# Attention of a two-layer streaming encoder: the reciprocal row sums are repeated on ScalarE and transposed as one block

## What is computed

```python
def sink_softmax(logits, sink):
    m = jnp.maximum(jnp.max(logits, axis=-1, keepdims=True), sink)
    p = jnp.exp(logits - m)
    return p / (jnp.sum(p, axis=-1, keepdims=True) + jnp.exp(sink - m))
...
    s_band = jnp.einsum('bnqcgd,bnscd->bncgqs', qb, kb).astype(jnp.float32) * scale + b_band
    s_band = jnp.where(valid[None, :, None, None, None, :], s_band, -jnp.inf)
```

## Time and profile before

| | |
|---|---|
| Runs | 2971.2 us median of 3 (2969.07 to 2971.53) |
| The profiled execution, its own time | 2970.41 us |
| Its span | 2968.6 us |
| TensorE products busy | 2883.8 us, 97% of the span |
| VectorE, ScalarE, GpSimd busy | 1532.7, 679.5 and 916.9 us |
| Attention of layer 0, of layer 1 | some 178 to 382 us, some 1632 to 1968 us from the start of the span |

### The profile page before, as it was taken

One profiled execution on the slowest core, in us unless ns is written; L12 is line 12 of the kernel. 1 busy time (PEld: TensorE's weight loads), 2 busy tenths in 40 slices (PEclk: granted clock), 3 DMA queues, 4 the chain that ended last, 5 costly groups with the idle time before them and its releaser, 6 DMA issues. The chain is left out here.

```text
span 2968.6 us, 47619 instructions
## 1 busy us (share of the span) xinstructions
PE 2883.8 (97%) x18423; PEld 2706.7 (91%) x18423; DVE 1532.7 (52%) x2815; ACT 679.5 (23%) x1327; POOL 916.9 (31%) x860
## 2 busy tenths in 40 slices
PE   8999999999999999999887999999999999999998
PEld 6987799999999999998487877789999999999997
DVE  5146624544444444455688777532644444444445
ACT  4035521000000000013467655532100000000002
POOL 4233333222222222224033754323222222222221
PEclk8999999999999999999999999999999999999998
DMA  4430011111111111114012000021111111111111
GB/s 123 66 96 10 22 29 36 36 36 42 42 42 42 42 42 42 36 43 130 1 35 72 11 10 9 20 80 37 37 42 42 42 37 41 42 42 38 39 36 74
DMA packets 178204, 129.78 MB, mean 44 GB/s; under 512 B 25313, under 2 KB 168353, under 8 KB 177846
## 3 DMA queue, kind: packets, MB, share of 16 engines
q1 hardware_dynamic: 178066, 127.90, 15.2%
HBM read 111.13 MB, written 15.16 MB: 43 GB/s over the span
## 5 line engine op out<-in xcount | busy, mean ns | idle before, releaser
L1215 POOL CAST w_hi<-w_raw 128x1024 fp32r<-128x1024 f32 x120 | 145.1, 1209 | 1111.8 <-PE ps_gemm L1450 606.9
L666 DVE TENSOR_TENSOR h<-h,ps_gemm 128x1170 f32<-128x1170 f32 x192 | 263.7, 1373 | 398.1 <-PE ps_gemm L1466 210.6
L1450 PE MATMUL ps_gemm<-xh,w_hi 128*128 128x390 f32 x1920 | 448.5, 341 | 0.0
L1450 PE MATMUL ps_gemm<-xh,w_lo 128*128 128x390 f32 x1920 | 448.1, 342 | 0.0
L1450 PE MATMUL ps_gemm<-xl,w_hi 128*128 128x390 f32 x1920 | 446.1, 340 | 0.0
L1450 PEld LDWEIGHTS ps_gemm<-xh,w_hi 128*128 128x128 f32 x1920 | 352.2, 189 | 0.1
L1450 PEld LDWEIGHTS ps_gemm<-xl,w_hi 128*128 128x128 f32 x1920 | 349.4, 189 | 0.0
L1450 PEld LDWEIGHTS ps_gemm<-xh,w_lo 128*128 128x128 f32 x1920 | 349.1, 189 | 0.0
L1218 POOL TENSOR_TENSOR w_lo<-w_raw,w_hi 128x1024 fp32r<-128x1024 f32 x120 | 289.5, 2413 | 17.4
L674 ACT ACTIVATE ac<-ac 128x1184 f32<-128x1184 f32 x44 | 52.5, 1194 | 863.2 <-DVE ac L731 863.2
L1414 PE MATMUL ps_gemm<-xl,w_hi 128*128 128x390 f32 x1056 | 246.5, 342 | 0.0
(11 more groups left out here) (411 smaller groups left out, 4716.1 us busy)
## 6 DMA issues: line engine op xcount, KB each, us to landing
w_raw<-in_w_gate SPq DMA_DIRECT2D x44, 512.0 KB, 3.8
w_raw<-in_w_up SPq DMA_DIRECT2D x44, 512.0 KB, 3.8
w_raw<-in_w_down SPq DMA_DIRECT2D x44, 512.0 KB, 3.5
w_raw<-in_w_in_b SPq DMA_DIRECT2D x13, 512.0 KB, 4.0
w_raw<-in_w_qkv_a SPq DMA_DIRECT2D x10, 512.0 KB, 4.0
residual_park<-h SPq DMA_DIRECT2D x1, 4680.0 KB, 13.6
h<-residual_park SPq DMA_DIRECT2D x8, 585.0 KB, 7.4
out<-yt SPq DMA_DIRECT2D x9, 512.0 KB
```

The costliest lines, as they stand in the source:

```text
L666: dve.tensor_tensor(c3(h[:, m, :]), c3(h[:, m, :]), pse(j), ALU.add).then_inc(evac[j % 2], 1)
L1215: pool.tensor_copy(whi[c % 3][:], raw[c % 2][:]).then_inc(w_hi_done, 1)
L1450: mm = pe.matmul(ps[j % 2][:, m_, 0:CH], w[:, k, :], x[:, k, m_ * CH:(m_ + 1) * CH], start=(k == 0 and w is wh and x is XH), stop=(k == KT ...
```

## The change

ScalarE gets a new instruction per unit: it repeats the two columns of reciprocals 64 times each into a tile of 128x128 (`ri_a` in layer 0, `ri_b` in layer 1, two buffers each), in step i+1 for unit i, between the first and the second exponential of unit i+1. TensorE transposes that tile as one block in place of the two products, and waits for `p_wide` in place of `p_rinv`. VectorE waits, before it overwrites reciprocals, for the copy made three units earlier. The five memsets of `ca` go from VectorE, step 4, to GpSimd, step 3, behind the sinks of unit 3 and ahead of the split of unit 0; VectorE waits for them at the end of step 7.

```diff
-             ("ptb_h", [P, 512], F32)],
+             ("ptb_h", [P, 512], F32), ("ri_b", [P, 2, 2, HD], F32)],
...
-             ("kts_a", [P, 2, 160], F32), ("sbias_a", [P, 2, 160], F32)],
+             ("kts_a", [P, 2, 160], F32), ("sbias_a", [P, 2, 160], F32), ("ri_a", [P, 2, 2, HD], F32)],
...
+        def inverse(layer, i):
+            return (hreg["ri_b"] if layer else x4["ri_a"])[:, i % 2, :, :]
...
+            def mask_windows():
+                ca = x12["ca"]
+                pool.wait_ge(ca_in, 32)
+                pool.memset(ca[:, :, BAND:BAND + 2 * META], 0.0).then_inc(ca_done, 1)
+                for o in (0, CW + META):
+                    pool.memset(ca[0:64, :, o + 192:o + 256], BIG).then_inc(ca_done, 1)
+                pool.wait_ge(ca_done, 6)
+                for o in (0, CW + META):
+                    pool.memset(ca[64:128, :, o:o + 64], BIG).then_inc(ca_done, 1)
+                pool.wait_ge(ca_done, 8)
...
                 if n < NU:
                     set_sinks(n)
+                if n == 3:
+                    mask_windows()
                 if n >= LAG + 1:
                     split_output(0, n - LAG - 1)
...
                         if b == "rinv":
-                            pe.wait_ge(p_rinv, NU * layer + i + 1)
-                            for r in range(2):
-                                mm = pe.matmul(tb[j % 2][HD * r:HD * (r + 1), P * k:P * (k + 1)],
-                                               stat(2, i, r).to_broadcast([P, HD]), ident[:], start=True, stop=True)
+                            pe.wait_ge(p_wide, NU * layer + i + 1)
+                            mm = pe.transpose(tb[j % 2][:, P * k:P * (k + 1)],
+                                              inverse(layer, i).rearrange("p r d -> p (r d)"), ident[:])
...
+                def repeat_inverse(i):
+                    act.wait_ge(p_rinv, NU * layer + i + 1)
+                    if i >= 2:
+                        act.wait_ge(p_tr, transposed(layer, i - 2))
+                    copy(inverse(layer, i), stat(2, i).unsqueeze(2).to_broadcast([P, 2, HD])).then_inc(p_wide, 1)
                 for n in range(NU + LAG):
                     parts = thirds(AT[layer][n])
                     part(parts[0])
                     if n < NU:
                         probs(n, 0)
                     part(parts[1])
+                    if 1 <= n <= NU:
+                        repeat_inverse(n - 1)
                     if n < NU:
                         probs(n, 1)
                     part(parts[2])
...
                         dve.wait_ge(p_exp, 2 * (NU * layer + n))
+                        if n >= 4:
+                            dve.wait_ge(p_wide, NU * layer + n - 3)
                         dve.reciprocal(stat(2, n - 1), stat(1, n - 1)).then_inc(p_rinv, 1)
...
             def mask_window(n):
+                if n == 7:
+                    dve.wait_ge(ca_done, 8)
                 if n == 8:
                     dve.wait_ge(sb_in, 16 * 32)
-                if n != 4:
-                    return
-                dve.wait_ge(ca_in, 32)
-                dve.memset(ca[:, :, BAND:BAND + 2 * META], 0.0).then_inc(ca_done, 1)
-                for o in (0, CW + META):
-                    dve.memset(ca[0:64, :, o + 192:o + 256], BIG).then_inc(ca_done, 1)
-                    dve.memset(ca[64:128, :, o:o + 64], BIG).then_inc(ca_done, 1)
-                dve.wait_ge(ca_done, 8)
```

More of the change, by code:

```diff
@@ L626, in build @@
         p_rinv = sem("pair_row_sum_inverse_done")
+        p_wide = sem("pair_inverse_repeated")
         p_tr = sem("pair_probs_transposed")
```

## The result

The changed kernel takes 2978.2 us in the median of 13 runs (2975.6 to 2980.5), the kernel before, run beside it, 2970.4 (2968.2 to 2972.0). The ratio is 1.0026 with a 95% interval of 1.0018 to 1.0034: 7.9 us slower. The forecast was 2965, 6 us faster, with 2955 to 2974.

What follows compares the result with a forecast made beforehand. TensorE, busy 97% of the span, was taken to bound the kernel. Terms -10 - 7 + 7.4 + 3 + 1 gave about -6 us, hence 2965 us against a median of 2971.2; range 2955 to 2974.

Steps and rivals of the forecast that it cites:

- First units of layer 0: Units 3 to 9: later masks and a loop through the copy, rounds of about 3.35 us; 7.4 us lost (4 to 9).
- a clock under 1.00: Sign against the forecast: granted clock below 1.00 in the two attention stretches; no size given.
- The block on TensorE: Attention units: one transposition replaces four instructions, 0.16 us less per unit; 10 us gained in layer 0, 7 in layer 1.
- no term is added for it: Attention units on TensorE: the gap at the change from 128 to 64 columns stands once in each order, so 0 us.
- ScalarE: Attention units: 146 added copies of 0.30 us, 44 us in all, mostly hidden; 1 us lost (0 to 3).
- First units of layer 1: Units 3 to 8: each round 0.58 us longer with the copy; 3 us lost (1.5 to 4).
- the dense stretches unchanged: Sign for the forecast: the dense layers outside the attention stretches keep their time, 0 us.
- The rival that came out slower: Attention units: the lone block overlaps with nothing and costs 0.26 us, no gain per unit; +11 us, 2982; chance 0.09.

Runs made afterwards that it cites:

- after + fill: Changed kernel plus unread TensorE products ahead of its wait for the copy in units 3 to 10 of layer 0: 2974.3 us, ratio 1.0019.
- both hybrids: Changed kernel, masks on VectorE, old product pair in first units of both layers, or of layer 0 only with copy ahead of exponential: 2962.0 us each.
- late split: Changed kernel with GpSimd splitting each unit's output in layer 0 one step later: 2977.3 us, ratio 1.0021.
- masks only: Kernel before with only the masks moved to GpSimd in step 3, old pair of products kept: 2975.8 us, ratio 1.0010.
- after, again: Changed kernel, unaltered, run again for a second profile: 2979.2 us, ratio 1.0031.
- block only, copy first: Changed kernel with masks back on VectorE and ScalarE's copy ahead of the next unit's first exponential: 2962.4 us, ratio 0.9958.
- block only: Changed kernel with the masks back on VectorE in step 4, copies and one block kept: 2976.1 us, ratio 1.0014.
- copies only: Kernel before plus ScalarE's 146 copies, which nobody reads; masks on VectorE, old pair of products: 2970.9 us, ratio 0.9999.

## Why the prediction was wrong

**First units of layer 0: the step that failed.** The mechanism was right: the copy is late, TensorE waits for it from unit 3 on, the masks end at 191.4 (forecast 191.7, with 2.3 us for the five memsets, not 2.6), and with the clock held (after + fill) a round takes 3.3 to 3.4 us, as forecast, and unit 9 is 8.0 us late against 7.4. The size was wrong, because that step added up rows of the kernel before, at a granted clock of 1.00, and kept that clock for a stretch in which it had itself put a TensorE wait of over 3 us. The fall to 0.50 made each round 4.0 to 4.3 us and the term 15.9 (13.6 in the second profile) in place of 7.4. The text listed a clock under 1.00 among the signs that would prove it wrong, but gave it no price and no rival.

In "TensorE: Matmul & The Clock Gate", section "HAM oscillation — how this bites in real kernels", the Trainium skill says that a TensorE wait can drop the clock, so that the work behind it starts at the low level. The trace agrees with its direction (the block behind the 3.17 us runs at 0.50); that it then stays low for 34 us with TensorE busy is this case's number.

**The block on TensorE.** 0.11 us per unit, not 0.16: -6.5 in layer 0 (60 steps, the forecast counts 63 units) and -5.6 in layer 1, not -10 and -7. Up to the first value product the estimate held (0.17). What failed is "no term is added for it": the change of columns stands once in either order, but it now lies right ahead of the value products, and these take 0.06 us longer. That the one makes the other was not tested.

**ScalarE.** The copy takes 0.296 us (forecast 0.30), and of 146 of them no cost shows (0.9999); the forecast's 1 us is too small to be told from that.

**First units of layer 1.** +3.6 in the profiled execution, forecast +3 (bounds 1.5 and 4). With the clock down there, as in two other profiles, it is 8.4.

**Between the layers.** The forecast had nothing here ("the dense stretches unchanged"); the two profiles of the changed kernel have 3.1 and 2.9 us. The VectorE instruction shown above takes 2.2 us, not 0.17, in all six profiles of kernels with both the block and the masks on GpSimd (+1.6 to +4.9 us between the layers) and, twice, in both hybrids (+2.9 and +2.8). In the nine profiles of the other eight kernels, the one before among them, it takes 0.17 (-0.4 to +0.8). So it goes with the program and not with the execution; why it takes longer, no run shows.

**Sum.** The measured rows add up to -6.5 - 5.6 + 15.9 + 3.6 + 3.1 = +10.5 us in the first profile, whose execution took 10.1 more than that of the kernel before, and with 13.6 and 2.9 to +8.0 in the second, which took 7.7 more; the median says +7.9. The second is 13.6 above the forecast's -5.6: 6.2 for the clock in layer 0's first units, 4.9 for the smaller gain per unit, 2.9 between the layers, 0.6 in layer 1's first units, less the 1 for ScalarE. So the clock is the largest miss, but only some half of it (8.5 of 16.1 in the first profile): with the clock held there the changed kernel still takes 2974.3. The rival that came out slower (2982) had the right sign for a reason that did not occur: the lone block does overlap.

## What to carry to other kernels

A new wait for TensorE has two prices, the wait and the clock behind it; read the granted clock of the very stretch in which the wait will lie, and price a fall to half there as a case of its own. An operation put on another engine's queue belongs ahead of what that engine waits for, if its own input is ready sooner: the same copy cost 3.6 us in the first units of layer 1 behind the exponential and gained 0.8 ahead of it. Where the gain per unit is 0.1 us, keep the change out of the units that have no slack, or fill the wait.

## What was not expected of the hardware

- The granted clock can stay at 0.50 for 34 us while TensorE shows no long wait (31.96 of 34 us busy); at 1.2 GHz the work of a unit lasts 3.8 us (late split) instead of 2.24, TensorE sets the pace, and the other engines have less to do (VectorE 11.08 us of the 34, before 20.82).
- The length of a wait doesn't tell by itself. In the first units of layer 0 the clock fell during or soon behind waits of 3.17, 2.45 (late split), 2.05 (masks only), 1.79 (after, again), 1.54 (block only, copy first), 1.17 (block only) and 0.92 us; it held at 1.10 (before, both hybrids), at 1.02 (copies only) and, behind sixteen unread products, at 1.19 (after + fill). Which execution falls also varies for one kernel: block only with copy first spread over 11 us. What decides it was not settled.
- An instruction of 6 columns on VectorE, far from the change, can take 2.2 us instead of 0.17 in every profile of some programs and in none of others.
- Unread products of some 0.12 us each went with a clock of 1.00 in six of the seven profiles that have them; in the seventh a wait of 0.92 us lay ahead of them.
